# Causal attention of a decoder trunk in pairs of heads, with the mask added by VectorE

## The reference, cut to what matters

```python
def causal_block_attention(q, k, v):          # T=512, 8 heads, dh=192, dv=128
    def one_block(args):                      # a block of 128 queries
        q_blk, blk = args
        s = jnp.einsum('bhqd,bhkd->bhqk', q_blk, kt) * scale
        q_pos = blk * Q_BLOCK + jnp.arange(Q_BLOCK)
        s = jnp.where(key_pos[None, :] <= q_pos[:, None], s, NEG_INF)
        p = jax.nn.softmax(s, axis=-1)
        return jnp.einsum('bhqk,bhkd->bhqd', p, vt)
```

## Time and profile before

| | us |
|---|---|
| median of 3 runs | 1632.45 |
| the runs | 1629.57, 1632.45, 1632.89 |
| the profiled execution | 1629.92 |
| its span, first to last instruction | 1628.1 |
| attention loop, first score to output projection | 928.3 to 1013.6 |
| its last scores read by VectorE | 1007.0 |
| output projection | 1013.6 to 1068.7 |
| routing and the first experts' start | 1068.7 to 1107 |
| experts of layer 1 to the end | 1107 to 1628 |

### The profile page before, as it was taken

How to read it: one execution, slowest core, us unless ns; L and a number is a source line. 1 busy time by engine, 2 the same in 40 slices (tenths; PEclk the granted TensorE clock), 3 DMA queues, 4 the chain that set the end, 5 groups by cost and what they waited for, 6 DMA issues and landing times.

```text
span 1628.1 us, 19431 instructions
## 1 busy us (share of the span) xinstructions
PE 1352.6 (83%) x6152; PEld 635.0 (39%) x6152; DVE 471.4 (29%) x928; ACT 294.7 (18%) x580; POOL 316.6 (19%) x427
## 2 busy tenths in 40 slices
PE   5988995997878787878789899977988787877886
PEld 4555453332323232323454576453333232322332
DVE  6997135111111111111614454152111111111114
ACT  3245111110101010100234543111111010010100
POOL 6313001222222222212000000002332222222120
PEclk8999996999999999998889899988999999999989
DMA  6513714999999999997420302266999999999996
GB/s 212 201 58 142 312 77 153 397 380 401 403 404 399 403 409 403 415 385 292 172 110 1 117 1 93 114 266 263 397 401 399 395 403 396 411 403 403 393 381 242
DMA packets 83524, 472.37 MB, mean 290 GB/s; under 512 B 13971, under 2 KB 16195, under 8 KB 32913
## 3 DMA queue, kind: packets, MB, share of 16 engines
q1 hardware_dynamic: 69792, 445.25, 69.1%
q0 software_dynamic: 11952, 20.14, 3.8%
q10 hardware_dynamic: 1728, 6.29, 1.0%
HBM read 454.59 MB, written 27.39 MB: 296 GB/s over the span
## 4 chain that ended last, share of the span: by engine, by line
PE 46%; SPq 31%; DVE 10%; issue 6%; DMA 5%; ACT 2%; DVEq 0%; POOL 0%; POOLq 0%; ACTq 0%
SPq L1628 20%; PE ps L1423 13%; SPq L1633 11%; PE ps L1443 6%; DMA ring<-in_moe_w 4%; PE ps L441 3%; PE ps L892 2%; PE ps L874 2%; PE ps L315 2%; PE ps L896 2%; PE ps L390 2%; PE ps L430 2%; PE ps L1413 2%; PE ps L927 2%; PE ps L925 1%
## 5 line engine op out<-in xcount | busy, mean ns | idle before, releaser
L1423 PE MATMUL ps<-ring,region_b 128*64 128x512 f32 x1408 | 345.1, 646 | 80.2 <-issue 54.5
L1423 PEld LDWEIGHTS ps<-ring,region_b 128*64 128x64 f32 x1408 | 117.0, 149 | 305.7 <-issue 268.6
L1560 DVE TENSOR_TENSOR extra<-extra,ps 128x256 f32<-128x256 f32 x64 | 26.9, 421 | 605.7 <-ACT extra L1498 575.2
L1423 PE MATMUL ps<-wbuf,region_b 128*64 128x512 f32 x320 | 161.8, 664 | 45.4 <-DMA region_a<-in_moe_w 29.8
L1443 PE MATMUL ps<-ring,extra 128*64 128x512 f32 x704 | 160.8, 598 | 34.2 <-DVE extra L1566 32.5
L1423 PE MATMUL ps<-region_a,region_b 128*64 128x512 f32 x320 | 162.0, 665 | 0.0
L1367 POOL DMA_INDIRECT region_b<-hrow,icol x120 | 111.2, 927 | 147.9 <-issue 147.9
L1379 POOL DMA_INDIRECT ytok<-extra,icol x120 | 105.6, 880 | 154.0 <-issue 154.0
L1498 ACT ACTIVATE extra<-ps 128x256 f32<-128x256 f32 x64 | 24.6, 384 | 589.5 <-PE ps L1423 581.6
L1573 DVE COPY extra<-ps 128x512 f32<-128x512 f32 x64 | 44.2, 691 | 241.3 <-PE ps L1443 241.3
L1423 PEld LDWEIGHTS ps<-wbuf,region_b 128*64 128x64 f32 x320 | 47.2, 152 | 154.4 <-issue 142.6
(11 more groups left out here) (308 smaller groups left out, 1601.9 us busy)
## 6 DMA issues: line engine op xcount, KB each, us to landing
ring<-in_moe_w SPq DMA_DIRECT2D x264, 1024.0 KB
wbuf<-in_moe_w SPq DMA_DIRECT2D x80, 1024.0 KB
region_a<-in_moe_w SPq DMA_DIRECT2D x40, 1024.0 KB
ytok<-ring SPq DMA_DIRECT2D x8, 1024.0 KB, 10.2
wbuf<-in_ev_w_in SPq DMA_DIRECT2D x3, 2048.0 KB, 17.8
wbuf<-in_ev_w_out SPq DMA_DIRECT2D x2, 2048.0 KB, 14.4
hrow<-region_a ACTq DMA_DIRECT2D x8, 512.0 KB, 10.7
region_a<-ytok SPq DMA_DIRECT2D x8, 512.0 KB, 5.4
```

The costliest lines, as they stand in the source:

```text
L1423: last = TE.matmul(ps[CAP * g:CAP * (g + 1), 2 + j, :], xtr[j][:, k, CAP * g:CAP * (g + 1)], up_weights(2 * slot + g, k), start=k == 0, st ...
```

## The change

The loop of TensorE goes over pairs g of steps (n = 2g and 2g+1):

- The two nope products come first, then the two rotary products one right behind the other: the even head's in rows 0 to 63, the odd head's in rows 64 to 127, into different banks.
- The product that added the mask is gone. VectorE adds the mask to the last 128 columns in PSUM, in place, before it takes the maximum.
- Scores go over four banks (0, 1, 2, 7) instead of three; scores of step n wait for the exponentials of n-4.
- The transposes are those of pair g-2, the value products those of pair g-3. ScalarE copies the transposed probabilities of step n-4 behind the exponential of step n. VectorE copies an output of four heads at n = 10, 14, ... instead of 8, 12, ...
- Six buffers for probabilities instead of three, four for the transposed instead of two.

```diff
-        pr = [r3[:, 4096:4608], extra[:, 2240:2752], r3[:, 4608:5120]]
-        pT = [extra[:, 2752:3264], extra[:, 3264:3776]]
+        pr = [r3[:, 4096 + i * 512:4608 + i * 512] for i in range(4)] + [sq[:, i * 512:(i + 1) * 512] for i in range(2)]
+        pT = [extra[:, 2240 + i * 512:2752 + i * 512] for i in range(3)] + [sq[:, 1024:1536]]
+        SBANK = (0, 1, 2, 7)
...
-            for n in range(NHD + 3):
-                if n < NHD:
-                    c, i = n // H, n % H
-                    if n >= 3:
-                        TE.wait_ge(s_ex, n - 2)
-                    o = ps[:, n % 3, 0:nk]
-                    TE.matmul(o, qTn[:, i, cc], kTn[:, i, 0:nk], start=True, stop=False)
-                    TE.matmul(ps[:, n % 3, nk - P:nk], ident, mask, start=False, stop=False)
-                    TE.matmul(o, qTr[r, i // 2, cc], kTr[r, i // 2, 0:nk], start=False, stop=True)\
-                        .then_inc(s_sc, 1)
-                m = n - 2
...
-                m = n - 3
+            for g in range(NHD // 2 + 3):
+                if g < NHD // 2:
+                    for n in (2 * g, 2 * g + 1):
+                        if n >= 4:
+                            TE.wait_ge(s_ex, n - 3)
+                        TE.matmul(ps[:, SBANK[n % 4], 0:nk], qTn[:, n % H, cc], kTn[:, n % H, 0:nk],
+                                  start=True, stop=False)
+                    for n in (2 * g, 2 * g + 1):
+                        r = slice(64 * (n % 2), 64 * (n % 2) + 64)
+                        TE.matmul(ps[:, SBANK[n % 4], 0:nk], qTr[r, n % H // 2, cc], kTr[r, n % H // 2, 0:nk],
+                                  start=False, stop=True).then_inc(s_sc, 1)
+                for m in (2 * g - 4, 2 * g - 3):
+                    if 0 <= m < NHD:
+                        TE.wait_ge(s_pn, m + 1)
+                        if m >= 2:
+                            TE.wait_ge(s_pte, m - 1)
...
+                for m in (2 * g - 6, 2 * g - 5):
+                    if m >= 0:
+                        TE.wait_ge(s_pte, m + 1)
...
-                    if n >= 3:
-                        S.wait_ge(s_pt, n - 2)
-                m = n - 2
+                    if n >= 6:
+                        S.wait_ge(s_pt, n - 5)
+                m = n - 4
...
-                    vlink(V.reduce_max(mx[:, b:b + 1], ps[:, b, 0:nk], AX.X))
+                    bank = ps[:, SBANK[n % 4], :]
+                    tt(bank[:, nk - P:nk], bank[:, nk - P:nk], mask, ALU.add)
+                    vlink(V.reduce_max(mx[:, b:b + 1], bank[:, 0:nk], AX.X))
```

More of the change, by code:

```diff
@@ L915, in odd_tensor @@
             NHD = H * TC
-            for n in range(NHD + 3):
-                if n < NHD:
-                    c, i = n // H, n % H
+            for g in range(NHD // 2 + 3):
+                if g < NHD // 2:
+                    c = 2 * g // H
                     nk = (c + 1) * P
-                    if n >= 3:
-                        TE.wait_ge(s_ex, n - 2)
-                    r = slice(64 * (i % 2), 64 * (i % 2) + 64)
                     cc = slice(c * P, (c + 1) * P)
-                    o = ps[:, n % 3, 0:nk]
-                    TE.matmul(o, qTn[:, i, cc], kTn[:, i, 0:nk], start=True, stop=False)
-                    TE.matmul(ps[:, n % 3, nk - P:nk], ident, mask, start=False, stop=False)
-                    TE.matmul(o, qTr[r, i // 2, cc], kTr[r, i // 2, 0:nk], start=False, stop=True)\
-                        .then_inc(s_sc, 1)
-                m = n - 2
[L930 to L937, removed]
-                m = n - 3
[L939 to L948, removed]
@@ new lines, in odd_tensor @@
+                for m in (2 * g - 4, 2 * g - 3):
[3 more added lines that the diff above has]
+                            TE.wait_ge(s_pte, m - 1)
+                        for b in range(m // H + 1):
+                            last = TE.transpose(ps[:, 3 + m % 2, b * P:(b + 1) * P],
+                                                pr[m % 6][:, b * P:(b + 1) * P], ident)
+                        last.then_inc(s_pt, 1)
@@ new lines, in odd_tensor @@
+                for m in (2 * g - 6, 2 * g - 5):
+                    if m >= 0:
+                        c, i = m // H, m % H
+                        if m % 4 == 0 and m >= 8:
+                            TE.wait_ge(s_oe, m // 4 - 1)
+                        TE.wait_ge(s_pte, m + 1)
+                        for b in range(c + 1):
+                            last = TE.matmul(ps[:, 5 + (m // 4) % 2, (m % 4) * P:(m % 4 + 1) * P],
+                                             vbuf[:, b, i * VD:(i + 1) * VD],
+                                             pT[m % 4][:, b * P:(b + 1) * P], start=b == 0, stop=b == c)
+                        last.then_inc(s_o, 1)
@@ L1022, in odd_scalar @@
                     keys_root(c + 1)
-            for n in range(H * TC + 2):
+            for n in range(H * TC + 4):
                 if n < H * TC:
@@ L1026, in odd_scalar @@
                     S.wait_ge(s_mx, n + 1)
-                    if n >= 3:
-                        S.wait_ge(s_pt, n - 2)
-                    S.activation(pr[n % 3][:, 0:nk], ps[:, n % 3, 0:nk], ACT.Exp, scale=scl[:, n:n + 1],
+                    if n >= 6:
+                        S.wait_ge(s_pt, n - 5)
+                    S.activation(pr[n % 6][:, 0:nk], ps[:, SBANK[n % 4], 0:nk], ACT.Exp, scale=scl[:, n:n + 1],
                                  bias=nb[:, n % 3:n % 3 + 1], accum_out=rs[:, n % 3:n % 3 + 1]).then_inc(s_ex, 1)
-                m = n - 2
+                m = n - 4
                 if m >= 0:
@@ L1034, in odd_scalar @@
                     S.wait_ge(s_pt, m + 1)
-                    if m >= 2:
-                        S.wait_ge(s_o, m - 1)
-                    S.activation(pT[m % 2][:, 0:nk], ps[:, 3 + m % 2, 0:nk], ACT.Copy).then_inc(s_pte, 1)
+                    if m >= 4:
+                        S.wait_ge(s_o, m - 3)
+                    S.activation(pT[m % 4][:, 0:nk], ps[:, 3 + m % 2, 0:nk], ACT.Copy).then_inc(s_pte, 1)
         def odd_vector():
@@ L1116, in odd_vector @@
                 ts(nscl[:, 8 * c:8 * c + 8], hrs[:, 0:8], -ATT_SCALE, ALU.mult)
-            for n in range(H * TC + 5):
+            for n in range(H * TC + 7):
                 if n < H * TC:
@@ L1131, in odd_vector @@
                     nk = (m // H + 1) * P
-                    V.tensor_scalar(pr[b][:, 0:nk], pr[b][:, 0:nk], ri[:, b:b + 1], None, ALU.mult).then_inc(s_pn, 1)
-                if n >= 8 and n % 4 == 0:
-                    g = n // 4 - 2
+                    V.tensor_scalar(pr[m % 6][:, 0:nk], pr[m % 6][:, 0:nk], ri[:, b:b + 1], None, ALU.mult)\
+                        .then_inc(s_pn, 1)
+                if n >= 10 and n % 4 == 2:
+                    g = (n - 10) // 4
                     V.wait_ge(s_o, 4 * g + 4)
```

## The result

| | before | changed |
|---|---|---|
| median, us | 1632.45 | 1618.41 |
| all runs | 1629.57 to 1632.89 (5 runs) | 1616.08 to 1623.86 (5 runs) |
| the profiled execution, its span | 1629.92, 1628.1 | 1623.86, 1622.1 |
| ratio to before | | 0.9924, 95% interval 0.9902 to 0.9945 |

The kernel is 14.0 us faster by the medians, 1613.5 was forecast, and the time lies in the range. The profiled execution of the changed kernel is the slowest of its five, that of the kernel before is near its fastest, so the stages are compared and not the ends.

What follows compares the result with a forecast made beforehand. TensorE's list was taken to bound the attention loop; 21.2 us came off it, and summed by stage with VectorE's pace and the tail the loop gained 18. That gave 1611.9 or 1614.4, forecast 1613.5 us, range 1608 to 1623.

Steps and rivals of the forecast that it cites:

- TensorE's list bounds the loop, and what follows moves with it: Attention loop: TensorE's list, 21.2 us shorter, sets its length until another engine is late; later stages move one to one.
- Rotary products side by side: TensorE in the attention loop: opposite-half rotary products overlap fully, saving one of each pair, 8.6 us.
- The visit's 0.35: TensorE in the loop: a visit to half the rows costs 0.35 us beside its passes; 16 fewer save 5.6.
- VectorE's pace in chunk 0: Attention loop, chunk 0: VectorE is the bound at 1.17 us a head, with 0.32 for the mask.
- Chunks 2 and 3: Later attention loop: three pairs at 4.0 to 4.05 us, three at 4.93, one at 5.15; last scores at 984.5.
- Chunks 0 and 1: Early attention loop: VectorE's pace, 21.1 us, plus 1 us for the low clock; head 16 at 952.5.
- the sum: Attention loop added by stage: gain 18 us, projection starting at 995.4 against 1013.6.
- the circle: Loop: a pair's second transpose waits for ScalarE's copy behind an earlier exponential; 4.0 us a pair against TensorE's 3.6 in chunk 2.
- The tail: Behind the last scores: 9.8 us of transposes and values, 1.1 for output copy and wait, then the projection.
- The mask's move as a gain: Attention loop: mask passes leave TensorE's list, 7.0 us; VectorE's added work is hidden in chunks 2 and 3.
- the signs named: Trace checks: rotary passes in twos, mask addition 0.29 us; prediction wrong if, among others, clock is 0.50 beyond 945.
- The rival of the low clock: Loop: low through chunks 0 and 1, 1622, chance 0.07; or still low in chunk 2, 1640 to 1658, chance 0.03.

Runs made afterwards that it cites:

- e2: Changed kernel with both rotary products of a pair taken from rows 0 to 63, so they cannot overlap: 1624.42 us, ratio 0.9953.
- e3: Changed kernel with each head's rotary product again behind its own nope product: 1636.24 us, ratio 1.0031.
- e1: Changed kernel with ScalarE copying the transposed probabilities of step n-3, not n-4, behind the exponential of step n: 1612.55 us, ratio 0.9874.
- e4: Changed kernel with the mask again a product on TensorE and VectorE's addition gone: 1615.5 us, ratio 0.9894.
- e6: e1 with the mask back as a product on TensorE: 1615.4 us, ratio 0.9901.
- e5: Kernel before with one part of the change alone, the mask added by VectorE in PSUM: 1642.03 us, ratio 1.0050.
- e9: e5 with four extra unused TensorE products ahead of the loop: 1637.89 us, ratio 1.0041.
- e8: e3 with four extra unused TensorE products ahead of the loop: 1625.03 us, ratio 0.9988.
- e12: e11 with four extra unused TensorE products ahead of the loop: 1607.67 us, ratio 0.9858.
- e11: e1 with the mask as a TensorE product in chunk 0 alone, on VectorE in chunks 1 to 3: 1611.85 us, ratio 0.9882.
- e10: Kernel before with four extra unused TensorE products ahead of the loop: 1626.74 us, ratio 0.9974.

## Why the prediction was right, step by step

- **TensorE's list bounds the loop, and what follows moves with it: right.** Projection and routing kept their 85.8 us in every kernel. The experts' start did not keep its length: 19.5 us before, 19.0 to 22.5 in the others, so up to 3 us of a gain can go there. Most of the spread lies between the gather's issue and the first transposes of its rows, 5.3 to 8.0 us, the rest in the first products, whose mean clock is 0.76 to 0.87; why the rows come later is open, no run was made on it.
- **Rotary products side by side: right.** The Trainium skill ("TensorEngine Tiling (Array Packing)", Key Properties) says that tiles operate independently. The trace agrees for 64 rows by 128 columns with both outputs on the same partitions: four passes in 1.06 us, against 1.91 in one half (e2). The visit's 0.35 was right too (0.38 in e3 against e2).
- **VectorE's pace in chunk 0: right**, 1.17 forecast and 1.17 measured a head; the mask's addition 0.29, its lower bound. It does not hold to the chunk's end, where VectorE waited 2.01 us for TensorE.
- **Chunks 2 and 3: right.** From the maximum of head 16 to that of head 24 16.7 us (17.0 forecast), from 24 to 30 15.0 (15.0).
- **Chunks 0 and 1: 24.1 us forecast as 22.1.** From the first maximum (933.39) to that of head 16 (957.48). Chunk 0 took 11.1, and the sum had 9.0 and 1 for the clock; chunk 1 took 13.0 against 12.1. Mis-sized were the low clock (from the mask of head 6 to that of head 8 4.4 us passed, nearly all at the low level) and the circle, which was said to spare chunk 1 until its last pair: TensorE waited 0.68 us for the copy at the end of chunk 0, and 0.77 and 0.73 in the first pairs of chunk 1. Without the late copy (e1) the two chunks take 9.0 and 12.1, as in the sum.
- **The tail: 14.5 us from the last scores to the projection, forecast as 10.9.** This is the step that failed most. The sum took the tail for TensorE's list alone, although the circle stood in the same text: behind the last scores there are no further scores to fill the time until ScalarE reaches the copy. The pause of 1.74 us and the fall of the clock behind it make the difference; with the earlier copy (e1) the tail is 10.7 on this count, the list.
- **The mask's move as a gain: wrong over the loop beside the circle.** The sum had it as 0.44 a pair off TensorE's list in chunks 2 and 3. There it gives 2.5 us, but the rest of the loop is 3.0 better with the product, partly by the clock (e4). Without the circle it is worth 4.0 in chunks 1 to 3 and costs 1.8 in chunk 0 (e6 against e1, and e6 entered at the full clock).
- **The sum:** 18 forecast for the loop, 13.1 in the trace; the shortfall is 2.0 in chunks 0 and 1 and 3.6 in the tail, less 0.3 that chunks 2 and 3 were quicker. The whole kernel gained 14.0 by the medians and 6.1 by the two spans, so the end did not move one to one. Without the late copy the loop gains 21.0 (e1). Of the signs named, the clock was at 0.50 beyond 945 after all, from 994.85 to 998.27.
- **The rival of the low clock** had 0.10 in its two forms and a larger share of the truth: it did not come to the changed kernel for long, but close relatives of it ran low through all of chunk 1 (e5, e9) or most of it (e3) and became slower than the kernel before.

What stays open is why the clock stays low in e3, e5 and e9 and not in the kernel before, with TensorE's row full in all. The lists differ in what stands between the half-row products: in the kernel before a mask product on all rows, in the changed kernel four nope passes and one visit for two heads. That these keep the clock is a reading of these cases, not shown; and the list alone does not decide, since e8 has that of e3 and stayed at 1.00 in its trace.

## What to carry to other kernels

Where a step is moved back by one more stage, look at every engine's list for what now stands ahead of the piece that the next stage waits for: here a copy behind an exponential that it did not need cost up to 8 us of the loop, a part of them by the clock, and one number in ScalarE's loop gave them back. Put two half-row products in opposite halves right behind each other; that alone was worth 5.7 us up to the last scores here. And work out the bound by stage before moving work between engines: here the mask belongs to VectorE in chunks 1 to 3, and in chunk 0 to TensorE when the clock is at full (6.9 us in e12; at the low clock 10.1 in e11 against 9.2 in e1).

## What the runs showed of the hardware that was not expected

- TensorE's row can be full and the clock stay low for tens of microseconds: 34.1 us in e9 and 42.6 us of the loop in e5, with 27 to 32 passes in 10 us where the full clock gave 50 (e5). The busy column does not tell; the clock column does.
- Less work on the bounding engine made the program slower (e5, +0.5%), and four useless products made it faster (e10, -0.3%).
- The clock fell behind pauses of TensorE of 0.2 to 0.6 us in chunk 0 (e9), and behind one of 1.74 us in the tail of the changed kernel, which then cost another 1.3 us on sixteen passes. It did not fall behind pauses of 0.87 us in chunk 0 of e8, 1.11 us in the tail of e2 and 1.30 us in that of e4: the length of one pause does not tell, and no run settles what does.
